# Summing two blocks of an adaLN projection on TensorE instead of VectorE in the first stage of a transformer block

## The chip, the cores and the metric

The kernel runs on one NeuronCore of a Trainium2 chip. It uses its engines TensorE (PE, matrix products into PSUM, with PEld for the loading of weights), VectorE (DVE), ScalarE (ACT), GpSimd (POOL) and SyncE (SP, which here issues nearly all DMA transfers). The metric is the device time of one execution in microseconds; the median of three runs is given. The profiler's trace is of one further execution.

## The reference

One layer of a hybrid encoder, batch 1, 512 tokens, 2048 features, everything in float32. From the conditioning vector c (2048 values) a modulation is computed, and the normalised input is scaled and shifted with it:

```python
c_act = jax.nn.silu(c)
mod = (c_act @ w_ada[i] + b_ada[i])[:, None, :]          # w_ada: 2048 x 12288
shift_m, scale_m, gate_m, shift_f, scale_f, gate_f = jnp.split(mod, 6, axis=-1)
h = rmsnorm(x, g_pre_mix[i]) * (1.0 + scale_m) + shift_m
y = token_mixer(h, w_in[i], ...)        # proj = h @ w_in, FoX attention + gated linear attention, @ w_out
x = x + gate_m * rmsnorm(y, g_post_mix[i])
h = rmsnorm(x, g_pre_mlp[i]) * (1.0 + scale_f) + shift_f
y = squared_relu_mlp(h, w_mlp_in[i], w_mlp_out[i])
x = x + gate_f * rmsnorm(y, g_post_mlp[i])
```

The change concerns scale_m and shift_m, 2048 columns of w_ada each, and the transpose of the normalised x.

## The kernel before

**The whole.** Each engine runs its own instruction list, written out by hand in one function per engine; semaphores order them. After a first stage the projection h @ w_in is computed in groups of six (later five) output tiles. Each float32 product is made of three matmuls on halves of the operands ("hi" and "lo", `split_mm`, lines 847 to 849). A group walks over 16 steps k, one for each 128 features. In a step TensorE makes 18 matmuls, and in a "slot" ahead of step k it does side work (`start_slot(2 * k)` in the first group). Later groups hold the attention in their slots; then follow the output projection and the MLP.

**The first stage, up to the first group.** SyncE issues in a fixed order: c, x in four token blocks, then w_ada in items (`load_am`, line 658), with weights of w_in between them. An item is 512 rows by 512 columns of w_ada, 1 MB in two transfers. Four items make a block of 512 columns. Blocks 0 to 3 are scale_m, blocks 4 to 7 shift_m, 32 items in all. Items lie in four buffers `am_item`; item n goes to buffer n % 4, so its load waits until item n - 4 is used (semaphore `am_used`). The first group's weights are loaded between items 18 and 31.

**Summing a block.** A matrix-vector product c_act @ w_ada is needed. DVE multiplies each row tile of an item with its column of c_act and adds it up in `am_acc` and `am_odd` (`add_am`, line 2094: 16 products and one sum, 17 instructions per block, `AM_BLOCK`). This leaves 128 partial rows. TensorE adds them over the partitions with a column of ones (`sum_columns`, line 1032), and DVE adds the bias (`mod_columns`, line 2158), which gives scale or shift for 512 features.

**x.** ScalarE squares each token block, GpSimd takes the inverse root, DVE scales blocks 0 to 2 and half of block 3, ScalarE the other half. Then TensorE transposes x, tile by tile (line 1020): all four token blocks of tile k into a PSUM bank (six banks, `TILES`), and ScalarE copies the bank to `xn_t` (line 1472).

**The fill.** While blocks of scale arrive one after the other, TensorE already computes the query part of the gated linear attention with the scale alone (`fill_unit`, line 1056). With it go the gate tiles (`gate_tiles`, line 1048): four matmuls at a time, each with 32 weight columns, each into its own 32 partitions of the bank BB, that is on four column strips of the array. The fill of block b needs scale block b.

**The first group.** It needs the last fill tile copied away, w_hi and w_lo of the first weights, and the modulated input of step k, so shift block k // 4. DVE's list there is: item 20, columns of block 4, item 21, `first_lo(0)` (line 2152), `modulated_pair(0)`, item 22 and so on (lines 2206 to 2240). Blocks 5, 6 and 7 of shift are summed in the slots 6, 14 and 22, ahead of the steps 3, 7 and 11; slot 28 holds the gate sums (lines 1095 to 1099).

Of the kernel before, what the change touches and what calls it, by code (L numbers as in the profile page):

```python
# [37 lines left out]
ALU = mybir.AluOpType  # L38
ACT = mybir.ActivationFunctionType
AX_X = mybir.AxisListType.X  # L40

P = 128
# [3 lines left out]
def build_block(nc, x, c, w_ada, b_ada, g_pre_mix, g_post_mix, w_in, b_fgate, w_gla_a2, b_gla_a2,  # L46
                g_fox_out, g_gla_out, w_out, g_pre_mlp, g_post_mlp, w_mlp_in, w_mlp_out, out):
    _, SEQ, D = x.shape
    KT = D // P
    TB = SEQ // P  # L50
# [22 lines left out]
    TILES = 6  # L73
# [21 lines left out]
    S_BLOCKS = KT // 4  # L95
    M_BLOCKS = 2 * S_BLOCKS
    F_ITEMS, G_ITEMS = KT // 2, KT // 4
    AM_BLOCK = 17
    F_USED = AM_BLOCK * M_BLOCKS
    G_USED = F_USED + FOX_GROUPS * F_ITEMS  # L100
    F_IN = 32 * M_BLOCKS
    G_IN = F_IN + 32 * FOX_GROUPS * F_ITEMS // 2
# [11 lines left out]
    with ExitStack() as ctx:  # L114
# [17 lines left out]
        x_raw = at("x_raw", [P, TB, D], R_A + 32 * KIB)  # L132
        x_junk = at("x_junk", [P, D], R_A)
        xn_t = at("xn_t", [P, KT, SEQ], R_B)
# [21 lines left out]
        am_item = [at(f"am_item{s}", [P, 4, 512], (R_AD, R_AD + 8 * KIB, R_G, R_G + 8 * KIB)[s]) for s in range(4)]  # L156
        am_acc = [at(f"am_acc{s}", [P, 512], (R_T + 12 * KIB, R_T + 14 * KIB, R_C + 6 * KIB)[s]) for s in range(3)]
# [342 lines left out]
        WARM_FILL = 10  # L500

        def items_used(n):
            return AM_BLOCK * (n // 4) + 4 * (n % 4)

        SPLIT_UNITS = (1, 3, 5, 7)

# [39 lines left out]
        def _(sp):  # L546
# [109 lines left out]


            def load_am(n):
                if n >= 4:
                    sp.wait_ge(am_used, items_used(n - 3))  # L660
                block, i = divmod(n, 4)
                col = (SCALE_M, SHIFT_M)[block // S_BLOCKS] + block % S_BLOCKS * 512
                for half in range(2):
                    k = 4 * i + 2 * half
                    sp.dma_start(am_item[n % 4][:, 2 * half:2 * half + 2, :], w_ada_t[:, k:k + 2, col:col + 512])\  # L665
                        .then_inc(am_in[n % 4], 16)
# [29 lines left out]
            def load_cumb(f):  # L696
                sp.wait_ge(ev_act, 3 * f + 1)
                for n in range(2):
                    sp.dma_start(cumb[n][:, :], cum_dram[bass.ds(2 * f + n, 1), :].to_broadcast([P, SEQ]))\
                        .then_inc(cumb_in, 16)  # L700

            F_AT = {0: (0,), 1: (1,), 2: (2, 3), 4: (4,), 5: (5,), 6: (6,), 7: (7,)}
            G_AT = {0: 0, 1: 1, 4: 2, 5: 3}

# [139 lines left out]
        def _(pe):  # L844
# [172 lines left out]
            pe.wait_ge(rows_in, 16 * 9)  # L1017
            pe.transpose(bank[5][:, 0:6 * KT], rows_a[:, :], ident[0:6 * KT, 0:6 * KT])
            pe.transpose(bank[5][:, 128:148], rows_b[:, :], ident[0:20, 0:20]).then_inc(rows_steps, 1)
            for k in range(KT):  # L1020
                if k == 0:
                    pe.wait_ge(xn_ready, TB)
                    pe.wait_ge(rows_steps, COLS_READY)
                if k == KT // 2:
                    pe.wait_ge(xn_right, 1)
                if k >= TILES:
                    pe.wait_ge(xt_act, k - TILES + 1)
                for t in range(TB):
                    last = pe.transpose(bank[k % TILES][:, t * P:t * P + P], x_raw[:, t, k * P:k * P + P], ident[:, :])
                last.then_inc(x_tr, 1)  # L1030

            def sum_columns(block):
                pe.wait_ge(am_used, items_used(4 * block + 4))
                if block:
                    pe.wait_ge(am_col, block)
                for j in range(4):
                    col = block // S_BLOCKS * 4 + j
                    last = pe.matmul(BA[:, col:col + 1], am_acc[block % 3][:, j * P:j * P + P], ones[:, 0:1],
                                     start=True, stop=True)
                last.then_inc(am_sum, 1)  # L1040

            sum_columns(0)
            for _ in range(WARM_FILL):
                pe.transpose(BB[:, 0:P], ident[:, :], ident[:, :])
            pe.wait_ge(xt_act, KT)
            FILL_SUMS = {3: 1, 7: 2, 11: 3, 14: S_BLOCKS}

            def gate_tiles(block):
# [33 lines left out]
            for block in range(S_BLOCKS):  # L1082
                pe.wait_ge(fill_in[block], 64)
                fill_unit(2 * block)
                fill_unit(2 * block + 1)

            FOX_SUMS = {6: S_BLOCKS + 1, 14: S_BLOCKS + 2, 22: S_BLOCKS + 3}

            def start_slot(s):
                if s in FOX_SUMS:  # L1090
                    sum_columns(FOX_SUMS[s])
                if s == 28:
                    pe.wait_ge(c_steps, C_ACT)
                    pe.wait_ge(gates_out, GATES_OUT)
                    pe.matmul(BB[0:32, :], gate_sel[:, :], gate_parts[:, :], start=True, stop=True)
                    pe.matmul(BB[32:40, :], gate_sel[:, RANK:RANK + FOX_HEADS], gate_parts[:, :], start=True, stop=True)
                    pe.wait_ge(g_ready, 1)
                    pe.matmul(BA[0:32, 8:9], g_sum[:, :], ones[:, 0:1], start=True, stop=True)
                    pe.matmul(BA[32:40, 8:9], g_sum[:, RANK:RANK + FOX_HEADS], ones[:, 0:1], start=True, stop=True)\
                        .then_inc(misc_sum, 1)  # L1100
# [214 lines left out]
        def _(act):  # L1315
# [143 lines left out]
            def scale_left(t):  # L1459
                cols = slice(0, D // 2)  # L1460
                act.wait_ge(x_rstd, t + 1)
                act.activation(x_raw[:, t, cols], x_raw[:, t, cols], ACT.Copy, scale=rstd[:, t:t + 1]).then_inc(xn_ready, 1)

            for t in range(TB):
                act.wait_ge(x_in[t], 16)
# [2 lines left out]
                act.activation(x_junk[:, :], x_raw[:, t, :], ACT.Square, accum_out=ss[:, t:t + 1]).then_inc(x_ss, 1)  # L1468
            scale_left(TB - 1)
            for k in range(KT):  # L1470
                act.wait_ge(x_tr, k + 1)
                act.activation(xn_t[:, k, :], bank[k % TILES][:, :], ACT.Copy).then_inc(xt_act, 1)

            def fill_operand(k):
                act.wait_ge(am_col, k // 4 + 1)
# [337 lines left out]
        def _(dve):  # L1813
# [280 lines left out]
            def add_am(n):  # L2094
                block, i = divmod(n, 4)
                total = am_acc[block % 3]
                dve.wait_ge(am_in[n % 4], 32 * (n // 4 + 1))
                if i == 0 and block >= 3:
                    dve.wait_ge(am_sum, block - 2)
                for j in range(4):  # L2100
                    part = (total, am_odd)[j % 2][:, :]
                    item, c_k = am_item[n % 4][:, j, :], c_act[:, 4 * i + j:4 * i + j + 1]
                    if i or j > 1 or (j and block):
                        dve.wait_ge(am_used, items_used(n) + j - 1)
                    if i or j > 1:
                        dve.scalar_tensor_tensor(part, item, c_k, part, ALU.mult, ALU.add).then_inc(am_used, 1)  # L2106
                    else:
                        dve.tensor_scalar(part, item, c_k, None, ALU.mult).then_inc(am_used, 1)
                if i == 3:
                    dve.wait_ge(am_used, items_used(n) + 4)  # L2110
                    dve.tensor_tensor(total[:, :], total[:, :], am_odd[:, :], ALU.add).then_inc(am_used, 1)
# [61 lines left out]
            def add_items(first, end):  # L2173
                for n in range(first, end):
                    add_am(n)
# [4 lines left out]

            scale_x(1)
            scale_x(2)
            add_am(0)
            scale_right(TB - 1)
            add_items(1, 4)
            mod_columns(0)
            fill_weights_lo(1)
            add_items(4, 6)
# [33 lines left out]
            add_am(27)  # L2222
            split_lo(4, 0, group_view)
            mod_columns(S_BLOCKS + 2)
            add_am(28)
            modulated_pair(8)
            add_items(29, 31)
            split_lo(5, 1, group_view)
            modulated_pair(10)
            add_am(31)  # L2230
            mod_columns(S_BLOCKS + 3)
            split_lo(6, 0, group_view)
            modulated_pair(12)
# [560 lines left out]
```

## Time and profile before

| | |
|---|---|
| median of three runs | 2189.64 us (2188.1 to 2189.9) |
| the profiled execution | 2188.36 us, span 2186.6 us |
| TensorE busy | 2152.3 us (98%) |
| DVE busy | 1545.3 us (71%) |
| ScalarE busy | 880.5 us (40%) |
| GpSimd busy | 362.9 us (17%) |
| moved by DMA | 445.46 MB, mean 204 GB/s |

The span is the profiled stretch; the execution's own time is 1.8 us longer. Busy shares are means over the whole span. Stages differ: in the first 100 us TensorE waits a good part of the time and the DMA engines are loaded, later it is the other way round. The views below therefore go by stretches and by waits. In a timeline a line gives start, duration, engine, line of the kernel, operation, output and inputs, shapes and count (x8: eight instructions merged; the duration is then that of them all), and in brackets the engine's idle time before it and what ended that. A float32 matmul shows as two matmul instructions, so a call to `pe.matmul` with float32 operands counts twice. A matmul's own duration holds its latency; the spacing of starts is what a matmul costs.

### The profile page before, as it was taken

The page shows a single profiled execution, that of the slowest core. Times are in us where ns is not written, and L with a number is a line of the kernel's source. Part 1 is how long each engine was busy: PE and PEld are TensorE (multiplying, and loading weights), DVE is VectorE, ACT ScalarE, POOL GpSimd, SP SyncE. Part 2 cuts the span into 40 slices and gives each one's busy share as a digit, 9 for nine tenths or more (in the row PEclk, how much of TensorE's full clock was granted, in tenths as well). Part 3 has the DMA queues.
Part 4 walks back from the last instruction along what each step waited for, and adds up shares of the span by engine and source line. Part 5 has one row for each costly group of instructions (what it writes and reads, how often), then busy time and mean ns, then how long its engine had stood idle before and what let it go on. Part 6 is the DMA issues. An engine that isn't in the chain of part 4 may idle for free.

```text
span 2186.6 us, 26836 instructions
## 1 busy us (share of the span) xinstructions
PE 2152.3 (98%) x9837; PEld 1754.0 (80%) x9837; DVE 1545.3 (71%) x1625; ACT 880.5 (40%) x1130; POOL 362.9 (17%) x206
## 2 busy tenths in 40 slices
PE   6999999999999999999999999999999999999998
PEld 4588888887777888888888888888888888888886
DVE  7987667677887626744554465445789898898988
ACT  5353333332343225543533434435444444444443
POOL 1000000000000001000000000000036455453634
PEclk9999999999999999999999999999999999999999
DMA  9966657655444443665675666655374765577764
GB/s 362 354 222 227 206 169 236 206 168 173 146 145 161 138 173 125 236 207 179 204 242 183 207 207 231 207 184 187 116 264 147 244 212 197 172 242 242 243 217 168
DMA packets 259333, 445.46 MB, mean 204 GB/s; under 512 B 18380, under 2 KB 102672, under 8 KB 253592
## 3 DMA queue, kind: packets, MB, share of 16 engines
q1 hardware_dynamic: 258976, 443.91, 60.5%
q8 instruction: 71, 1.16, 0.2%
q14 instruction: 38, 0.31, 0.0%
q10 hardware_dynamic: 248, 0.08, 0.0%
HBM read 384.14 MB, written 59.79 MB: 203 GB/s over the span
## 4 chain that ended last, share of the span: by engine, by line
PE 94%; DMA 2%; DVE 2%; issue 1%; SPq 1%; ACT 0%; DVEq 0%; POOL 0%; POOLq 0%
PE pair L847 30%; PE pair L849 30%; PE pair L848 30%; DMA am_item<-in_w_ada 2%; PE pair L948 1%; PE pair L922 1%; DVE am_acc L2106 0%; SPq L665 0%; DVE am_odd L2106 0%; PE pair L939 0%; PE pair L988 0%; PE pair L997 0%; PE pair L1151 0%; PE pair L889 0%; ACT y L1619 0%
## 5 line engine op out<-in xcount | busy, mean ns | idle before, releaser
L847 PE MATMUL pair<-in_hi,w_hi 128*128 128x512 f32 (+1 forms) x1728 | 689.6, 399 | 2.9 <-DVE in_lo L2134 2.8
L849 PE MATMUL pair<-in_hi,w_lo 128*128 128x512 f32 (+1 forms) x1728 | 670.9, 388 | 0.0
L848 PE MATMUL pair<-in_lo,w_hi 128*128 128x512 f32 (+1 forms) x1728 | 669.9, 388 | 0.0
L847 PEld LDWEIGHTS pair<-in_hi,w_hi 128*128 128x128 f32 x1728 | 324.7, 188 | 73.7 <-issue 10.1
L849 PEld LDWEIGHTS pair<-in_hi,w_lo 128*128 128x128 f32 x1728 | 324.4, 188 | 68.2
L848 PEld LDWEIGHTS pair<-in_lo,w_hi 128*128 128x128 f32 x1728 | 325.0, 188 | 64.8 <-issue 1.9
L847 PE MATMUL pair<-v_op,hid_r 128*128 128x512 f32 x896 | 348.7, 389 | 0.3 <-issue 0.3
L849 PE MATMUL pair<-v_op,hid_r 128*128 128x512 f32 x896 | 348.6, 389 | 0.0
L848 PE MATMUL pair<-v_op,hid_r 128*128 128x512 f32 x896 | 348.6, 389 | 0.0
L1826 DVE TENSOR_TENSOR w_lo<-w_raw,w_hi 128x2048 fp32r<-128x2048 f32 x62 | 144.7, 2334 | 287.5 <-ACT w_hi L1329 287.5
L2487 DVE TENSOR_TENSOR v_op<-v_raw,v_op 128x1024 fp32r<-128x1024 f32 x192 | 295.6, 1561 | 64.5 <-ACT v_op L1785 63.5
L1785 ACT ACTIVATE v_op<-v_raw 128x1024 fp32r<-128x1024 f32 x192 | 203.3, 1061 | 286.0 <-PE pair L849 268.0
L1329 ACT ACTIVATE w_hi<-w_raw 128x2048 fp32r<-128x2048 f32 x63 | 120.5, 1912 | 228.3 <-PE pair L849 228.3
L2752 POOL TENSOR_TENSOR v_sum<-v_raw,v_raw 128x512 f32<-128x512 f32 x60 | 149.2, 2513 | 367.8 <-DVE v_raw L2502 367.8
L847 PEld LDWEIGHTS pair<-v_op,hid_r 128*128 128x128 f32 x896 | 168.2, 188 | 35.8 <-ACT v_op L1785 0.7
L849 PEld LDWEIGHTS pair<-v_op,hid_r 128*128 128x128 f32 x896 | 168.2, 188 | 34.9
L848 PEld LDWEIGHTS pair<-v_op,hid_r 128*128 128x128 f32 x896 | 168.2, 188 | 34.9
L1818 DVE TENSOR_TENSOR w_lo<-w_raw,w_hi 128x1536 fp32r<-128x1536 f32 (+2 forms) x78 | 137.2, 1759 | 74.9 <-ACT w_hi L1320 74.0
L1320 ACT ACTIVATE w_hi<-w_raw 128x1536 fp32r<-128x1536 f32 (+2 forms) x78 | 116.0, 1487 | 177.6 <-PE pair L849 170.0
L2761 POOL TENSOR_TENSOR v_raw<-v_raw,v_sum 128x512 f32<-128x512 f32 x60 | 135.4, 2288 | 18.4 <-DVE v_op L2487 18.4
L2673 POOL TENSOR_TENSOR ada<-ada,c_act 128x2048 f32<-128x2048 f32 x8 | 31.4, 3926 | 587.8 <-DMA ada<-in_w_ada 552.4
L2543 DVE TENSOR_TENSOR y_t<-pair,y_t 128x1024 f32<-128x1024 f32 x104 | 125.0, 1215 | 0.7 <-PE pair L849 0.7
(283 smaller groups left out, 2289.5 us busy)
## 6 DMA issues: line engine op xcount, KB each, us to landing
w_raw<-in_w_mlp_in SPq DMA_DIRECT2D x64, 1024.0 KB, 5.3
v_raw<-in_w_mlp_out SPq DMA_DIRECT2D x128, 512.0 KB, 5.0
hid_r<-hid_scratch SPq DMA_DIRECT2D x112, 512.0 KB, 6.5
hid_scratch<-hid_r SPq DMA_DIRECT2D x28, 1792.0 KB, 8.3
am_item<-in_w_ada SPq DMA_DIRECT2D x64, 512.0 KB, 8.6
af_item<-in_w_ada SPq DMA_DIRECT2D x64, 512.0 KB, 4.7
w_raw<-in_w_in SPq DMA_DIRECT2D x96, 256.0 KB, 3.5
w_raw<-in_w_in SPq DMA_DIRECT2D x160, 128.0 KB, 3.4
```

Of the source, the lines that this page charges most:

```text
L847: pe.matmul(dst, a[0], b[0], start=start, stop=False, skip_group_check=onto)
L848: pe.matmul(dst, a[0], b[1], start=False, stop=False, skip_group_check=onto)
L849: return pe.matmul(dst, a[1], b[0], start=False, stop=stop, skip_group_check=onto)
L1320: act.activation(view(w_hi[n]), view(w_raw[n]), ACT.Copy).then_inc(hi_done, 1)
L1329: act.activation(m1_hi[m1_slot(j)][:, :], w_raw[j % 2][:, :], ACT.Copy).then_inc(hi_done, 1)
L1785: act.activation(v_op[i % 4][:, 0, :], raw_of(u, p)[:, h, :], ACT.Copy).then_inc(v_hi, 1)
L1818: dve.tensor_tensor(view(w_lo[n]), view(w_raw[n]), view(w_hi[n]).bitcast(F32), ALU.subtract)\
L1826: dve.tensor_tensor(m1_lo[m1_slot(j)][:, :], w_raw[j % 2][:, :], m1_hi[m1_slot(j)][:, :].bitcast(F32), ALU.subtract).then_inc(lo_done, 1)
L2487: dve.tensor_tensor(v_op[i % 4][:, 1, :], raw_of(u, p)[:, h, :], v_op[i % 4][:, 0, :].bitcast(F32), ALU.subtract).then_inc(v_lo, 1)
L2543: return dve.tensor_tensor(dst, src[:, :, :], dst, ALU.add)
L2752: last = pool.tensor_tensor(v_sum[:, h, cols], v_raw[q[B22]][:, h, cols], v_raw[q[B11]][:, h, cols], ALU.add)
L2761: last = pool.tensor_tensor(b21, b21, v_sum[:, h, cols], ALU.subtract)
```

## The change

Three edits belong together.

- **Blocks 0 and 7 are summed by TensorE** (`strip_sums`). For item i of the block it makes four matmuls, one for each row tile: the weights are one column of c_act repeated 32 times, the moving operand is the row tile (128 x 512 of float32). Row tile j goes to column strip j, partitions 32 j to 32 j + 31 of BB; the four items add up in PSUM. DVE then copies BB to `am_acc`, times 1/32 (`strips_out`), since each strip holds 32 equal rows, and `sum_columns` and `mod_columns` go on as before. DVE's products for items 0 to 3 and 28 to 31 are gone.
- **x is transposed by token blocks.** TensorE transposes token blocks 0 to 2 of the first six tiles as soon as each block is scaled. The last token block, and all four of the later tiles, follow. The sets for items 0, 1 and 2 stand ahead of tiles 0, 4 and 9, that for item 3 behind tile 15. Tiles 5, 7, 9, 11 and 13 are copied by DVE, the others by ScalarE.
- **Block 7** (items 28 to 31): the sets stand in the slots 16, 18 and 20 (two) of the first group, ahead of steps 8, 9 and 10. DVE copies them out behind `modulated_pair(10)`.

The buffers' waits follow: items 4 to 7 wait for the sets (`am0_used`) in place of DVE, and SyncE waits for all eight sets before it goes on to group 1. The order in which it issues is as it was. `am0_used` and `am0_sum` are further counts on semaphores already there.

```diff
-    F_USED = AM_BLOCK * M_BLOCKS
+    F_USED = AM_BLOCK * (M_BLOCKS - 2)
...
+        XT_DVE = (5, 7, 9, 11, 13)
...
             def load_am(n):
-                if n >= 4:
+                if n >= 8:
                     sp.wait_ge(am_used, items_used(n - 3))
+                elif n >= 4:
+                    sp.wait_ge(am0_used, AM0_USED + n - 3)
...
+            sp.wait_ge(am0_used, AM0_USED + 8)
...
+            def x_transpose(k, t):
+                return pe.transpose(bank[k % TILES][:, t * P:t * P + P], x_raw[:, t, k * P:k * P + P], ident[:, :])
+
+            def strip_sums(i, last_block=False):
+                if i == 0 and last_block:
+                    pe.wait_ge(gates_out, GATES_OUT)
+                elif i == 0:
+                    pe.wait_ge(c_steps, C_ACT)
+                pe.wait_ge(am_in[i], 32 * M_BLOCKS if last_block else 32)
+                for j in range(4):
+                    k = 4 * i + j
+                    last = pe.matmul(BB[32 * j:32 * j + 32, :], c_act[:, k:k + 1].to_broadcast([P, 32]),
+                                     am_item[i][:, j, :], start=(i == 0), stop=(i == 3))
+                last.then_inc(am0_used, 1)
+
+            for t in range(TB - 1):
+                pe.wait_ge(xn_ready, t + 1)
+                if t == 0:
+                    pe.wait_ge(rows_steps, COLS_READY)
+                for k in range(TILES):
+                    x_transpose(k, t)
+            SUMS_AHEAD = {0: 0, 4: 1, 9: 2}
             for k in range(KT):
+                if k in SUMS_AHEAD:
+                    strip_sums(SUMS_AHEAD[k])
...
                 if k >= TILES:
-                    pe.wait_ge(xt_act, k - TILES + 1)
-                for t in range(TB):
-                    last = pe.transpose(bank[k % TILES][:, t * P:t * P + P], x_raw[:, t, k * P:k * P + P], ident[:, :])
-                last.then_inc(x_tr, 1)
+                    xt_copied(pe, k - TILES)
+                    for t in range(TB - 1):
+                        x_transpose(k, t)
+                x_transpose(k, TB - 1).then_inc(x_tr, 1)
+            strip_sums(3)
...
+            STRIPS = {16: (0,), 18: (1,), 20: (2, 3)}
...
             def start_slot(s):
+                for i in STRIPS.get(s, ()):
+                    strip_sums(i, last_block=True)
                 if s in FOX_SUMS:
                     sum_columns(FOX_SUMS[s])
...
-            add_am(0)
             scale_right(TB - 1)
-            add_items(1, 4)
+            for k in XT_DVE:
+                dve.wait_ge(x_tr, k + 1)
+                dve.tensor_copy(xn_t[:, k, :], bank[k % TILES][:, :]).then_inc(xn_right, 1)
+            def strips_out(block, n):
+                dve.wait_ge(am0_used, AM0_USED + 4 * n)
+                dve.tensor_scalar(am_acc[block % 3][:, :], BB[:, :], 1.0 / 32, None, ALU.mult).then_inc(am0_sum, 1)
+
+            strips_out(0, 1)
             mod_columns(0)
...
-            add_am(28)
             modulated_pair(8)
-            add_items(29, 31)
             split_lo(5, 1, group_view)
             modulated_pair(10)
-            add_am(31)
+            dve.wait_ge(am_sum, S_BLOCKS + 1)
+            strips_out(M_BLOCKS - 1, 2)
             mod_columns(S_BLOCKS + 3)
```

## Rows read from the trace of the kernel before

**Rows 1.** busy time of the engines over the whole span, of the page (share, instructions)

```profile
PE 2152.3 (98%) x9837; PEld 1754.0 (80%) x9837; DVE 1545.3 (71%) x1625; ACT 880.5 (40%) x1130; POOL 362.9 (17%) x206
```

**Rows 2.** TensorE's waits from 98 us to the end: us in total, times, longest

```profile
PE pair L847 <- DVE in_lo L2134: 2.8, 1, 2.8
PE pair L1151 <- DVE y L2322: 0.5, 1, 0.5
```

**Rows 3.** chain of waits from 76 to 98.6 us: start, us, what

```profile
82.16 0.40 SPq L665
...
82.60 10.12 DMA am_item<-in_w_ada
...
92.74 0.75 DVE am_acc L2106
...
95.40 1.75 DVE w_lo L2155
97.15 0.61 DVE in_lo L2134
...
98.01 0.47 PE pair L847
```

**Rows 4.** stretches of 5 us: busy per engine, TensorE's clock, DMA share, GB/s

```profile
5.00:10.00 5.00, 0.00 (x0) 0.00 (x0) 0.60 (x3) 3.83 (x5) 0.21 (x2) 1.00 1.01 413
...
45.00:50.00 5.00, 5.00 (x15) 3.52 (x14) 3.37 (x7) 3.60 (x6) 0.00 (x0) 0.66 1.05 386
...
90.00:95.00 5.00, 5.00 (x24) 3.98 (x22) 4.20 (x9) 4.79 (x7) 0.00 (x0) 1.00 1.05 387
95.00:100.00 5.00, 2.24 (x11) 1.70 (x10) 5.00 (x7) 4.47 (x8) 0.00 (x0) 1.00 0.55 175
```

**Rows 5.** tile am_item to 170 us, what ended DVE's idle time (us, times)

```profile
  DMA am_item<-in_w_ada: 3.9, 7
```

**Rows 6.** timeline of all engines up to the first fill block

```profile
16.72 0.49 DVE L2108 TENSOR_SCALAR am_acc<-am_item,c_act 128x512 f32<-128x512 f32 x1 [0.70 <-DMA am_item<-in_w_ada]
...
18.48 8.90 PE L1029 MATMUL pair<-ident,x_raw 128*128 128x128 f32 x64 [6.84 <-ACT x_raw L1462]
...
25.13 0.75 DVE L2106 SCALAR_TENSOR_TENSOR am_acc<-am_item,c_act,am_acc 128x512 f32<-128x512 f32 x1 [0.24 <-DMA am_item<-in_w_ada]
...
28.40 1.19 ACT L1500 ACTIVATE fill_hi<-fill_w 128x1024 fp32r<-128x1024 f32 x1
28.65 1.05 PE L1038 MATMUL pair<-ones,am_acc 128*128 128x1 f32 x8 [1.27 <-DVE am_acc L2111]
...
30.18 2.56 ACT L1476 ACTIVATE in_tmp<-xn_t,mod_a 128x512 f32<-128x512 f32 x4 [0.59 <-DVE mod_a L2169]
```

**Rows 7.** the same timeline, TensorE in the first fill block

```profile
31.05 3.67 PE L1075 MATMUL pair<-in_tmp,fill_w 128*128 128x512 f32 x8 [0.19 <-ACT in_tmp L1476]
...
34.65 1.07 PE L1052 MATMUL pair<-in_tmp,wm_raw 128*32 128x512 f32 x8
...
35.64 3.70 PE L1075 MATMUL pair<-in_tmp,fill_w 128*128 128x512 f32 x8
```

**Rows 8.** timeline of TensorE at the sums of block 7 and the gates

```profile
144.88 0.95 PE L1038 MATMUL pair<-ones,am_acc 128*128 128x1 f32 x8
...
157.84 0.39 PE L849 MATMUL pair<-in_hi,w_lo 128*128 128x512 f32 x1
158.16 0.62 PE L1095 MATMUL pair<-gate_parts,gate_sel 128*32 128x512 f32 x1
...
159.17 0.50 PE L847 MATMUL pair<-in_hi,w_hi 128*128 128x512 f32 x1
159.51 0.40 PE L848 MATMUL pair<-in_lo,w_hi 128*128 128x512 f32 x1
```

**Rows 9.** timeline of SyncE, the issue of item 31

```profile
130.49 0.94 SPq L665 DMA_DIRECT2D am_item<-in_w_ada  x2
```

**Rows 10.** timeline of DVE, a copy of a bank with a scalar

```profile
167.19 0.69 DVE L1836 TENSOR_SCALAR grp<-pair 128x512 f32<-128x512 f32 x1
```

More of the change, by code:

```diff
@@ L502, in items_used, with xt_copied @@
         def items_used(n):
-            return AM_BLOCK * (n // 4) + 4 * (n % 4)
+            return AM_BLOCK * (n // 4 - 1) + 4 * (n % 4)
+        am0_used, AM0_USED = c_in, 16
+        am0_sum, AM0_SUM = rows_in, 16 * 9 + 1
+        XT_DVE = (5, 7, 9, 11, 13)
+        x3_left = 1
+        def xt_copied(engine, k):
+            if k in XT_DVE:
+                engine.wait_ge(xn_right, 2 + XT_DVE.index(k))
+            else:
+                engine.wait_ge(xt_act, x3_left + len([n for n in range(k + 1) if n not in XT_DVE]))
         SPLIT_UNITS = (1, 3, 5, 7)
@@ L1019, in _ @@
             pe.transpose(bank[5][:, 128:148], rows_b[:, :], ident[0:20, 0:20]).then_inc(rows_steps, 1)
+            def x_transpose(k, t):
[18 more added lines that the diff above has]
+            SUMS_AHEAD = {0: 0, 4: 1, 9: 2}
             for k in range(KT):
+                if k in SUMS_AHEAD:
+                    strip_sums(SUMS_AHEAD[k])
                 if k == 0:
-                    pe.wait_ge(xn_ready, TB)
-                    pe.wait_ge(rows_steps, COLS_READY)
+                    pe.wait_ge(xt_act, x3_left)
                 if k == KT // 2:
@@ L1026, in _ @@
                 if k >= TILES:
-                    pe.wait_ge(xt_act, k - TILES + 1)
-                for t in range(TB):
-                    last = pe.transpose(bank[k % TILES][:, t * P:t * P + P], x_raw[:, t, k * P:k * P + P], ident[:, :])
-                last.then_inc(x_tr, 1)
-            def sum_columns(block):
-                pe.wait_ge(am_used, items_used(4 * block + 4))
+                    xt_copied(pe, k - TILES)
[3 more added lines that the diff above has]
+            strip_sums(3)
+            def sum_columns(block):
+                if block == 0:
+                    pe.wait_ge(am0_sum, AM0_SUM)
+                elif block == M_BLOCKS - 1:
+                    pe.wait_ge(am0_sum, AM0_SUM + 1)
+                else:
+                    pe.wait_ge(am_used, items_used(4 * block + 4))
                 if block:
@@ L1044, in _ @@
                 pe.transpose(BB[:, 0:P], ident[:, :], ident[:, :])
-            pe.wait_ge(xt_act, KT)
+            xt_copied(pe, KT - 1)
+            xt_copied(pe, XT_DVE[-1])
             FILL_SUMS = {3: 1, 7: 2, 11: 3, 14: S_BLOCKS}
@@ L1461, in scale_left @@
                 act.wait_ge(x_rstd, t + 1)
-                act.activation(x_raw[:, t, cols], x_raw[:, t, cols], ACT.Copy, scale=rstd[:, t:t + 1]).then_inc(xn_ready, 1)
+                act.activation(x_raw[:, t, cols], x_raw[:, t, cols], ACT.Copy, scale=rstd[:, t:t + 1]).then_inc(xt_act, 1)
             for t in range(TB):
@@ L1470, in _ @@
             for k in range(KT):
-                act.wait_ge(x_tr, k + 1)
-                act.activation(xn_t[:, k, :], bank[k % TILES][:, :], ACT.Copy).then_inc(xt_act, 1)
+                if k not in XT_DVE:
+                    act.wait_ge(x_tr, k + 1)
+                    act.activation(xn_t[:, k, :], bank[k % TILES][:, :], ACT.Copy).then_inc(xt_act, 1)
+            xt_copied(act, XT_DVE[-1])
             def fill_operand(k):
@@ L2102, in add_am @@
                     item, c_k = am_item[n % 4][:, j, :], c_act[:, 4 * i + j:4 * i + j + 1]
-                    if i or j > 1 or (j and block):
+                    if items_used(n) + j > 1:
                         dve.wait_ge(am_used, items_used(n) + j - 1)
```

## The prediction

> **What bounds the kernel now.** The page's busy row comes first: TensorE is busy for 2152.3 of 2186.6 us [rows 1]. Next the waits of TensorE from 98 us to the end: the 2.8 us at 98 are the only wait of weight, and from there on TensorE runs through [rows 2]. So the time is the start of that run (98.01 us) plus what TensorE has to do in it plus a tail. A change gains if it brings the start forward, and loses whatever it adds to TensorE behind it, one for one.
>
> What sets the start? The chain back from 98.01 reads: in_lo (DVE, 97.15), w_lo (95.40), the four products of block 5's item 21 from 92.74, that item's transfer of 10.12 us, and before it SyncE's issue at 82.16, released by DVE [rows 3]. Read quickly, this says that a quicker DVE would issue item 21 sooner and so land it sooner. The windows say otherwise: from 5 to 95 us the DMA share is at or above 1.01 in each of the 18 stretches of 5 us; 45:50 and 90:95 both show 1.05 at 386 and 387 GB/s, and only 95:100 falls to 0.55 [rows 4]. A transfer that takes 10.12 us while 387 GB/s flow has about 3.9 MB in front of it (itself included): it stands in a line that never empties. The order of the line is SyncE's program order, which the change leaves as it is. So item 21 lands at about 92.7 whatever DVE does earlier, and the order "item 21, first w_lo, first in_lo" on DVE stays too.
>
> **The change, part by part.**
>
> *Block 0 leaves DVE (items 0 to 3).* Before: item 0 is taken up at 16.72, item 3 at 25.13 on landing, the columns are summed by TensorE at 28.65, and ScalarE starts the fill operand at 30.18 [rows 6]. After: of the 64 transposes (8.90 us from 18.48, so 0.139 each [rows 6]) the 18 of token blocks 0 to 2 for the first six tiles lie in TensorE's idle time before 18.48, and so does the set for item 0, there at 16.72. The other 46 stay: 46 x 0.139 = 6.4 us. Among them stand the sets for items 1 to 3. The nearest row for a set is the gate tiles: the same four column strips, 512 columns of float32, eight instructions; from their start to the next matmul it is 35.64 - 34.65 = 0.99 us [rows 7]. A set that waits for its item holds the transposes behind it: from 16.72 to 25.13 the items come some 2.8 us apart, so item 2 at about 22.3, and TensorE is at its set after 18 transposes and a set, 18.48 + 2.5 + 0.99 = 22.0; it waits 0.3. Then DVE copies the sums out of PSUM; the nearest row is 0.69 us for 128x512 with a scalar [rows 10]. From 18.48: 6.4 + 3 x 0.99 + 0.3 + 0.69 = 10.4, so the column sums start at 28.9 against 28.65: no change to speak of. The earliest end is item 3's landing, 25.13 + 0.99 + 0.69 = 26.8, 1.8 us sooner; but the operands of the fill are only split from 28.40 [rows 6]. The late end, with sets and transposes at half speed, is 18.48 + 2 x 9.4 + 0.69 = 38. I take 28.9, since the speed of both is measured in this very stage.
>
> What either end is worth at 98 us: DVE waits 3.9 us in all for landings of these items, in seven places, of which 0.70 (item 0) and 0.24 (item 3) lie in block 0 [rows 5, 6]. The other 2.9 us lie between block 0 and the start. An earlier front lengthens these waits; a later one eats them first. So from 1.8 us early to 2.9 us late the start stays. Cost taken: 0.
>
> *Copies out of PSUM.* Five of sixteen go from ScalarE to DVE, which now has nothing else there; behind them only the 0.69 us copy waits. Nothing at 98 us.
>
> *Loads of items 4 to 7* wait for sets, not for DVE. The sets come in the same order and within about a microsecond of DVE's products, and the line in front of the DMA engines is some 10 us deep [rows 3]. Nothing. Were that cover gone, a late set for item 3 would delay item 7 by as much, still inside the 2.9 us.
>
> *Block 7 leaves DVE (items 28 to 31), and four sets go into the run that never waits.* DVE loses 17 instructions around 128 to 144 us, which nobody waits for [rows 2]. TensorE gets one set before step k = 8, one before k = 9, two before k = 10. A step takes (144.88 - 98.01 - 2 x 0.95) / 11 = 4.09 us [rows 3, 8], so a matmul 4.09 / 18 = 0.227. The cost of a change of form in this run is seen at the gate sums: after 157.84 the next start was due at 158.07 and came at 158.16 (0.09); behind them the first matmul took 159.51 - 159.17 = 0.34 in place of 0.227 (0.11) [rows 8]. A single set: 0.09 + 0.99 + 0.11 = 1.19; the double one 0.09 + 1.98 + 0.11 = 2.18. Sum: 2 x 1.19 + 2.18 = 4.56 us. The low end is 4 x 0.99 = 3.96; a gain is excluded because TensorE has no idle time there to be filled. The high end is four strips one after the other: four matmuls of 128 columns take 34.65 - 31.05 = 3.60 us in eight instructions [rows 7], four sets 14.4 us. I take 4.56: the gate tiles differ from a set only in that the 32 weight columns are one column repeated.
>
> The Trainium skill has a rule on packed tiles: its page "TensorE: Matmul & The Clock Gate" (section "Measured speedup vs the span model") gives 3.07 times for four packed tiles, where the rows here make 3.60 / 0.99 = 3.6 times. By that rule of the Trainium skill a set would be 3.60 / 3.07 = 1.17 and the sum, as an estimate, 5.3 us; the measured rows go first.
>
> *New waits there.* The double set waits for item 31, issued at 130.49 to 131.43 [rows 9]; even with 10.12 us to land it is there at 141.6. Step 10 starts at 144.88 - 4.09 = 140.8, plus two sets 143.2. The first set's wait for the gate sums is long past, as these are copied during the fill. Nothing. DVE waits for the double set before it copies; queued behind are block 7's columns, a w_lo and two in_lo, which in both kernels cannot start before the columns are summed at the head of step 11. That sum shifts with TensorE, so their distance to step 12 stays. SyncE's new wait for all sets ends around 145, before the first w_raw of group 1 is free, which takes the w_lo queued behind block 7's columns. Nothing.
>
> **The sum.** Start 0, run +4.56, tail 0. The profiled execution took 2188.36 us (span 2186.6), 1.28 below the median of the three runs, so it would become 2192.9; a median of runs should move with it: 2189.64 + 4.56 = 2194.2. That is 0.21%, right at what a measurement of this kernel can tell from no change (0.2%, 4.4 us).
>
> **Rivals.**
> 1. *The line of transfers has room: not slower.* If the rate would rise when SyncE is released sooner, DVE would no longer wait for landings: 2.9 us, plus at most 1.8 us from the front, brings the start 4.7 us forward, to 93.3 (the fill's own matmuls end at 98.01 - 2.8 = 95.2 [rows 2, 3], so 2.8 is what remains): +4.56 - 2.8 = +1.8, so 2191.4. For it: the chain, which goes through SyncE's wait. Against it: the share of 1.05 without a gap. The Trainium skill, page "DMA: Bandwidth & Descriptors" (section "Where 436 GB/s comes from"), puts the ceiling of the ports at 435 GB/s; worked out from that figure, 387 would leave 11% of room, as an estimate. The trace goes to 413 GB/s while x is loaded, at a share of 1.01, and to 387 at 1.05 with the items [rows 4], so here that room is not seen to be usable. To be faster than before by 0.2% the start would have to come 9 us sooner, before the fill can end.
> 2. *Strips don't run side by side.* With repeated weights, or four different moving operands, a set costs 3.60: +14.4 us, 2204. For: no row shows repeated weights. Against: the gate tiles' four operands differ as well.
> 3. *The front slips.* If sets and transposes ahead of the fill run at half speed for most of the time, block 0 is late by more than the 2.9 us of waits behind it; each microsecond beyond them comes on top. With 2 us beyond: 2196.2. For: TensorE's granted clock is 0.66 in 45:50 [rows 4], so this stage does lose speed. Against: that stretch costs the start nothing now.
> 4. *The change doesn't tell*: the sets would have to lie in idle time of TensorE from 132 to 145, and 2189.6 would stay. There is none [rows 2].
>
> **Chances.** Forecast 0.70 (own range 2193.0 to 2195.5), rival 1 0.14, rival 2 0.04, rival 3 0.10, rival 4 0.02. The range of 8 in 10 takes in most of rivals 1 and 3: 2190.2 to 2197.0. The forecast lies across the bound of 0.2%: 0.39 of it slower, 0.31 the same. Rivals 2 and 3 add 0.12 to slower and 0.02 to the same, rival 1 gives 0.11 to the same and 0.03 to faster, rival 4 0.02 to the same. Slower 0.51, same 0.46, faster 0.03; I give faster 0.05 for what I don't see, at the cost of the same.
>
> **What would show it.** Item 21 still lands near 92.7 and the run starts between 97.5 and 98.5 (rival 1: before 97, and DMA above 390 GB/s). Four sets in the run, each 0.9 to 1.2 us from its first start to the next in_hi matmul (rival 2: over 3). TensorE without a wait between 98 and 170. DVE idle for some 11 us in 128 to 146. The prediction is wrong if the start moves by over 1 us, or if a wait of TensorE appears behind a set.

## The result and the profile after

The changed kernel takes 2193.66 us, the median of 15 runs (2192.98 to 2195.37), against 2189.43 for the kernel before in the same comparison (15 runs, 2188.02 to 2190.31): ratio 1.0022, 95% interval 1.0015 to 1.0029. That is 4.23 us slower, where the prediction said 4.56 and 2194.2. The profiled execution has a span of 2191.2 us, 4.6 more than before.

Busy time of the engines from the page, which answers to [rows 1]: TensorE has 64 matmuls more, the eight sets of eight; DVE has 27 instructions less.

```profile
PE 2163.7 (99%) x9901; PEld 1755.2 (80%) x9901; DVE 1528.2 (70%) x1598; ACT 878.6 (40%) x1125; POOL 361.8 (17%) x206
```

TensorE's waits from 98 us on (total, times, longest), for [rows 2]. The start of the run is still released by in_lo on DVE, now after 2.0 us in place of 2.8. No wait stands behind a set. One of 0.5 us at L953, among the attention's matmuls later on, is new to the list.

```profile
PE pair L861 <- DVE in_lo L2184: 2.0, 1, 2.0
PE pair L953 <- ACT prob L1436: 0.5, 1, 0.5
```

The chain of waits from 76 to 98.6 us, for [rows 3]. It no longer passes through a transfer or SyncE: it comes through the fill on TensorE and reaches DVE's products of item 21. The step from TensorE to DVE at 94.49 is no wait, though: DVE's products start back to back there (93.83, 94.49) and DVE is not idle before them. The run still starts at 97.76 (before 98.01).

```profile
81.15 3.67 PE pair L1120 x8
...
94.49 0.75 DVE am_odd L2156
...
96.82 0.70 DVE in_lo L2184
...
97.76 0.47 PE pair L861
```

Stretches of TensorE's clock, DMA share and GB/s (the last three columns), for [rows 4]: the line of transfers is as full as it was, up to 95 us. New is the clock in the first fill block, 0.74 and 0.92, where the kernel before was granted 1.00 in both stretches; that one had its low stretch later (0.66 in 45:50), where the changed kernel has 1.00.

```profile
30.00:35.00 5.00, 4.78 (x21) 3.14 (x22) 3.81 (x8) 3.44 (x6) 0.00 (x0) 0.74 1.05 386
35.00:40.00 5.00, 5.00 (x17) 1.74 (x16) 3.59 (x6) 0.15 (x1) 0.00 (x0) 0.92 1.09 351
...
90.00:95.00 5.00, 5.00 (x25) 4.18 (x25) 4.85 (x10) 4.34 (x6) 0.00 (x0) 1.00 1.05 385
95.00:100.00 5.00, 3.02 (x14) 2.19 (x13) 5.00 (x7) 4.84 (x9) 0.00 (x0) 1.00 0.59 180
```

The timeline up to the first fill block, for [rows 6, 7] (start, length, engine and line, [idle before]). The sets of items 0 and 1 take 1.94 and 1.89 us, those of items 2 and 3 1.06. Six transposes at 16.06 take 1.54. The column sums stand at 30.03 (before 28.65), and the first half of the fill block takes 5.36 (before 3.67).

```profile
16.06 1.54 PE L1036 MATMUL pair<-ident,x_raw 128*128 128x128 f32 x6 [0.54 <-DVE x_raw L2165]
...
17.53 1.94 PE L1046 MATMUL pair<-am_item,c_act 128*32 128x512 f32 x8
...
20.44 1.89 PE L1046 MATMUL pair<-am_item,c_act 128*32 128x512 f32 x8
...
23.95 1.06 PE L1046 MATMUL pair<-am_item,c_act 128*32 128x512 f32 x8
...
28.15 1.06 PE L1046 MATMUL pair<-am_item,c_act 128*32 128x512 f32 x8
...
30.03 1.05 PE L1082 MATMUL pair<-ones,am_acc 128*128 128x1 f32 x8 [0.81 <-DVE am_acc L2239]
...
32.42 5.36 PE L1120 MATMUL pair<-in_tmp,fill_w 128*128 128x512 f32 x8 [0.18 <-ACT in_tmp L1526]
```

The tile am_item to 170 us, for [rows 5]: DVE no longer waits for any landing. Its line there (3.9 us, seven times) is gone, and no other has taken its place.

TensorE's timeline at the first and the last slot with sets and at the sums of block 7, for [rows 8]. A single set is 133.52 - 132.52 = 1.00 us to the next matmul, the double one 144.97 - 143.12 = 1.85. From the start of the run to the sums of block 7 it is 149.21 - 97.76 = 51.45 us; before it was 144.88 - 98.01 = 46.87.

```profile
132.20 0.39 PE L863 MATMUL pair<-in_hi,w_lo 128*128 128x512 f32 x1
132.52 1.06 PE L1046 MATMUL pair<-am_item,c_act 128*32 128x512 f32 x8
133.52 0.50 PE L861 MATMUL pair<-in_hi,w_hi 128*128 128x512 f32 x1
133.85 0.39 PE L862 MATMUL pair<-in_lo,w_hi 128*128 128x512 f32 x1
...
142.80 0.39 PE L863 MATMUL pair<-in_hi,w_lo 128*128 128x512 f32 x1
143.12 1.92 PE L1046 MATMUL pair<-am_item,c_act 128*32 128x512 f32 x16
144.97 0.50 PE L861 MATMUL pair<-in_hi,w_hi 128*128 128x512 f32 x1
145.31 0.40 PE L862 MATMUL pair<-in_lo,w_hi 128*128 128x512 f32 x1
...
149.21 0.94 PE L1082 MATMUL pair<-ones,am_acc 128*128 128x1 f32 x8
```

DVE's timeline. Its first in_lo waits 1.41 us for TensorE's fill, which it did not before, and the last sum of block 1 stands at 45.47. Item 21 is taken up at 92.49 without a wait for its landing. DVE idles 7.54 us before the copy of block 7's sums and 4.32 behind it.

```profile
38.84 1.29 DVE L2199 TENSOR_TENSOR in_lo<-in_tmp,in_hi 128x512 fp32r<-128x512 f32 x2 [1.41 <-PE pair L1097]
...
45.47 0.69 DVE L2161 TENSOR_TENSOR am_acc<-am_acc,am_odd 128x512 f32<-128x512 f32 x1
...
92.49 0.75 DVE L2156 SCALAR_TENSOR_TENSOR am_acc<-am_item,c_act,am_acc 128x512 f32<-128x512 f32 x1
...
145.18 0.69 DVE L2239 TENSOR_SCALAR am_acc<-pair 128x512 f32<-128x512 f32 x1 [7.54 <-PE pair L1046]
150.19 0.16 DVE L2221 TENSOR_TENSOR mod_b<-pair,cols_a 128x4 f32<-128x4 f32 x1 [4.32 <-PE pair L1082]
```

The same sum of block 1 in DVE's timeline of the kernel before:

```profile
42.88 0.69 DVE L2111 TENSOR_TENSOR am_acc<-am_acc,am_odd 128x512 f32<-128x512 f32 x1
```

### The profile page after: what moved, and what is told of

It is laid out like the page before. It is cut to its first block, busy times and chain, and to the rows that moved or that the text cites. A ratio compares the mean times of both kernels' runs of the same rounds, so it can differ in the third digit from the quotient of the medians.

```text
span 2191.2 us, 26931 instructions
## 1 busy us (share of the span) xinstructions
PE 2163.7 (99%) x9901; PEld 1755.2 (80%) x9901; DVE 1528.2 (70%) x1598; ACT 878.6 (40%) x1125; POOL 361.8 (17%) x206
## 4 chain that ended last, share of the span: by engine, by line
PE 96%; DVE 1%; issue 1%; ACT 1%; DMA 0%; DVEq 0%; POOL 0%; SPq 0%; POOLq 0%; ACTq 0%
PE pair L861 30%; PE pair L863 30%; PE pair L862 30%; PE pair L1120 1%; PE pair L962 1%; PE pair L936 1%; PE pair L1046 0%; PE pair L953 0%; PE pair L1002 0%; PE pair L1011 0%; PE pair L1036 0%; PE pair L1199 0%; PE pair L903 0%; PE pair L1082 0%; DMA w_raw<-in_w_in 0%
```

## The experiments

The theory: the start of the run is set by item 21's landing and the order on DVE behind it, so the relief of DVE at block 0 is worth nothing; the loss is the four sets of block 7, one for one. The rivals: the line of transfers has room and the start can be had by a quicker DVE; or the loss is in what the sets do to their neighbours, not in the sets.

**Each half alone.** Block 0 by sets and block 7 on DVE as before (against the changed kernel, its core):

```
-            STRIPS = {16: (0,), 18: (1,), 20: (2, 3)}
+            STRIPS = {}
...
+            add_am(28)
             modulated_pair(8)
+            add_items(29, 31)
             split_lo(5, 1, group_view)
             modulated_pair(10)
-            dve.wait_ge(am_sum, S_BLOCKS + 1)
-            strips_out(M_BLOCKS - 1, 2)
+            add_am(31)
```

> Only the first half of the change: block 0 by sets on TensorE with x transposed by token blocks; block 7 stays on DVE. Theory (the line of transfers sets the start of the run, the sets in the run are the whole loss): start between 97.5 and 98.3, TensorE's work in the run as before, so 2189.4 within 1 us of the kernel before. Rival (DVE's chain sets the start and block 0's relief is worth something): start 1.5 to 2.8 us earlier, 2186.6 to 2188. Second rival (the late front costs): start after 99, over 2190.5.

Measured: 2189.32 us, ratio 1.0001 (0.9992 to 1.001), span 2186.6 as before. The sets of items 0 and 1 are slow here too (1.94, 1.79), the column sums stand at 29.88, and the start at 97.76. The first half of the first fill block takes 3.67 us, as in the kernel before, and DVE still waits for item 21. TensorE's timeline, then DVE's:

```profile
32.27 3.67 PE L1118 MATMUL pair<-in_tmp,fill_w 128*128 128x512 f32 x8 [0.19 <-ACT in_tmp L1524]
```

```profile
92.49 0.75 DVE L2154 SCALAR_TENSOR_TENSOR am_acc<-am_item,c_act,am_acc 128x512 f32<-128x512 f32 x1 [0.32 <-DMA am_item<-in_w_ada]
```

Block 7 by sets, block 0 and the transposes as in the kernel before (against the changed kernel, its core):

```
             def load_am(n):
-                if n >= 8:
+                if n >= 4:
                     sp.wait_ge(am_used, items_used(n - 3))
-                elif n >= 4:
-                    sp.wait_ge(am0_used, AM0_USED + n - 3)
...
+            add_am(0)
             scale_right(TB - 1)
...
-            strips_out(0, 1)
+            add_items(1, 4)
```

> Only the second half: block 7 by four sets in the slots 16, 18 and 20, block 0 and the transposes as before. Theory: start at 98.0, sums of block 7 at 149.4 (144.88 + 4.56), time +4.6: 2194.0. Rival (the loss comes from the front or from something between): time within 1 us of before, and the loss in the run of the first half alone.

Measured: 2193.04 us, ratio 1.002 (1.0011 to 1.0029), span 2191.1. From its start at 97.85 to the sums of block 7 at 149.26 it is 51.41 us. Against the kernel before it is 4.5 us by the spans and 3.46 by the medians of this comparison. So the whole loss lies in block 7; block 0 neither adds to it nor takes from it by more than the interval of the first half, 0.1% or about 2 us, can show.

**Is it the landing?** Half the bytes of each item from item 4 on are left out:

```
-                    sp.dma_start(am_item[n % 4][:, 2 * half:2 * half + 2, :], w_ada_t[:, k:k + 2, col:col + 512])\
+                    rows = 1 if n >= 4 else 2
+                    sp.dma_start(am_item[n % 4][:, 2 * half:2 * half + rows, :], w_ada_t[:, k:k + rows, col:col + 512])\
```

> The kernel before, but from item 4 on each transfer of an item brings one row tile of its two, so half the bytes; all products are still made, half of them on rows left over from earlier items. Theory (a full line of transfers sets the start): items land earlier, DVE's 2.9 us of waits for landings between block 0 and the start vanish, and the start falls to 95 to 96. Rival (DVE's chain alone sets the start): 98.0 as before.

Measured: 2184.88 us in one run, with the kernel before at 2189.64 beside it. TensorE's timeline has the start 3.4 us sooner (a little below the 95 to 96 expected), still behind DVE:

```profile
94.65 0.47 PE L848 MATMUL pair<-in_hi,w_hi 128*128 128x512 f32 x1 [1.72 <-DVE in_lo L2135]
```

With half the bytes gone DVE has no wait for a landing behind block 0, so its own work is the next bound, some 3.4 us away. The weights stand in the same line and come sooner too, so this run moves more than item 21. The other side is a quicker DVE with the line as it is: two of four products of an item on 16 columns in place of 512, from item 4 on:

```
-                    part = (total, am_odd)[j % 2][:, :]
-                    item, c_k = am_item[n % 4][:, j, :], c_act[:, 4 * i + j:4 * i + j + 1]
+                    cols = slice(0, 16 if n >= 4 and j > 1 else 512)
+                    part = (total, am_odd)[j % 2][:, cols]
+                    item, c_k = am_item[n % 4][:, j, cols], c_act[:, 4 * i + j:4 * i + j + 1]
```

> The kernel before, but from item 4 on the products with the third and fourth row tile of an item take 16 of 512 columns, so DVE has about 1.1 us less to do per item, some 20 us before the start; the transfers are unchanged. Theory (the line sets the start): item 21 is taken up at 92.5 to 92.9, and the start is the landing plus the shorter work, 96.5 to 97.2. Rival (DVE's chain sets the start): item 21 is taken up well before 92, and the start comes at the end of the fill, 94 or earlier.

Measured: 2187.12 us in one run. DVE's waits for landings rise from 3.9 to 21.2 us, and its timeline shows item 21 taken up on landing, at nearly the same time as before (92.74). DVE's timeline, then TensorE's:

```profile
92.59 0.75 DVE L2107 SCALAR_TENSOR_TENSOR am_acc<-am_item,c_act,am_acc 128x512 f32<-128x512 f32 x1 [2.86 <-DMA am_item<-in_w_ada]
94.21 1.75 DVE L2156 TENSOR_TENSOR w_lo<-w_raw,w_hi 128x1536 fp32r<-128x1536 f32 x1
```

```profile
96.82 0.47 PE L847 MATMUL pair<-in_hi,w_hi 128*128 128x512 f32 x1 [1.10 <-ACT gg L1493]
```

The start, 96.82, comes 1.19 us sooner, as w_lo does (94.21 in place of 95.40): 0.15 of it is the landing, the rest what the shorter products of item 21 itself save. The row names ScalarE's copy of a fill tile as what ended the wait, so here the end of the fill would not have let the run start sooner either. A DVE that is quicker earlier waits longer and lands nothing sooner by more than 0.15 us: the prediction's reading against rival 1 holds.

**The order behind the landing.** In the kernel before, item 21 is put behind the first w_lo and the first in_lo:

```
-            add_am(21)
             first_lo(0)
-            modulated_pair(0)
+            modulated_lo(0)
+            add_am(21)
+            modulated_lo(1)
```

> The kernel before with one edit on DVE's list: item 21 is added up between the two first in_lo in place of ahead of the first w_lo, so the start no longer waits for that item's landing. Theory (landing of item 21 plus the work behind it on DVE sets the start): the start falls to the end of the fill and its copies, 95.2 to 95.8, time 2.2 to 2.8 us lower: 2186.6 to 2187.2. Rival (DVE has that much to do in any order): the start stays at 97.5 to 98, time as before.

Measured: 2186.53 us, ratio 0.9987 (0.9978 to 0.9996), span 2184.7: better than both kernels. TensorE's timeline: the fill and the run join without a wait; a smaller one of 0.88 us appears 18 us later, and the sums of block 7 stand 1.78 us sooner than before.

```profile
94.72 0.39 PE L849 MATMUL pair<-in_hi,fill_lo 128*128 128x512 f32 x1
94.95 0.39 PE L847 MATMUL pair<-in_hi,w_hi 128*128 128x512 f32 x1
...
113.49 0.47 PE L847 MATMUL pair<-in_hi,w_hi 128*128 128x512 f32 x1 [0.88 <-DVE in_lo L2134]
...
143.10 0.94 PE L1038 MATMUL pair<-ones,am_acc 128*128 128x1 f32 x8
```

The same move on the kernel with block 0 by sets (against the first experiment; the same lines):

```
-            add_am(21)
             first_lo(0)
-            modulated_pair(0)
+            modulated_lo(0)
+            add_am(21)
+            modulated_lo(1)
```

> The first half of the change (block 0 by sets, block 7 on DVE) together with item 21 between the two first in_lo. Theory: block 0's relief adds nothing to the reordering; start 95.2 to 96, time 2186.6 to 2187.6, the same as the reordering alone. Rival (relief of DVE shows once the landing is out of the way): 1 us or more below the reordering alone.

Measured: 2187.53 us, ratio 0.9991 (0.9982 to 1.0), span 2186.0; the first matmul of the run at 95.72, the sums of block 7 at 143.74. With the landing out of the way, the late front is no longer free: it costs 143.74 - 143.10 = 0.64 us, since the fill itself ends later (its last matmul starts at 95.50, against 94.72).

And on the changed kernel:

```
-            add_am(21)
             first_lo(0)
-            modulated_pair(0)
+            modulated_lo(0)
+            add_am(21)
+            modulated_lo(1)
```

> The changed kernel with item 21 of block 5 put behind the first w_lo and the first in_lo on DVE, nothing else. Theory (start of the run and the sets in it add up): the start of the run comes forward as in the kernel before with the same move (there the time fell by 2.9 us of its 2189.4, the sums of block 7 by 1.8 us), less up to 1 us since the front with sets is late by 1.4 us; the four sets still cost 4.6 us: 2191.0 to 2192.0. Rival (the two share a cause): the time falls to that of the kernel before or below, under 2189.7, or doesn't fall, over 2193.

Measured: 2192.51 us, ratio 1.0017 (1.0008 to 1.0026), half a microsecond above the range expected; its profiled execution took 2191.85. The sums of block 7 stand at 148.26, 4.52 us behind the 143.74 of the kernel without sets in the run. So the order moves the start, the sets cost their time behind it, and the two add. The order gains less on the changed kernel, though: 1.15 us by the medians and 1.2 by the spans, against 3.05 and 1.9 in the kernel before.

**The front at full speed.** Transposes of the unit matrix, 62 in all (the expectation counts 67), keep TensorE busy ahead of the sets (against the changed kernel, its core):

```
+            def warm(n):
+                for _ in range(n):
+                    pe.transpose(BA[:, 0:P], ident[:, :], ident[:, :])
...
+            warm(36)
...
+                warm((6, 5, 10)[t])
...
+            warm(5)
```

> The changed kernel with 67 transposes of the identity in TensorE's idle time ahead of the sets for items 0 and 1, so that it is busy from about 3 us on. Theory (the front does not matter, and it came late because those sets ran at half speed): each set takes about 1.0 us, block 0's column sums start at 28.2 to 28.6 in place of 30.03, DVE waits for landings again, and the start stays at 97.5 to 98. Rival (the late front set the start in the changed kernel): start 1.5 us earlier.

Measured: 2193.98 us in one run. The sets take 1.06 us each, but the column sums come at 29.37, not 28.2 to 28.6, because the set of item 2 waited for its landing; and the start slipped to 99.35, which no theory had. TensorE's timeline, then DVE's:

```profile
23.29 1.07 PE L1052 MATMUL pair<-am_item,c_act 128*32 128x512 f32 x8 [1.27 <-DMA am_item<-in_w_ada]
...
97.83 0.39 PE L863 MATMUL pair<-in_hi,fill_lo 128*128 128x512 f32 x1
...
99.35 0.47 PE L861 MATMUL pair<-in_hi,w_hi 128*128 128x512 f32 x1 [1.14 <-ACT gg L1551]
```

```profile
94.09 0.75 DVE L2164 SCALAR_TENSOR_TENSOR am_acc<-am_item,c_act,am_acc 128x512 f32<-128x512 f32 x1 [0.21 <-DMA am_item<-in_w_ada]
```

Item 21 was taken up 1.6 us later here, on landing, and the start came 1.6 us later. That does not show that the start followed the landing: the last matmul of the fill started at 97.83, against 95.40 in the changed kernel, and the row of the start names ScalarE's copy of a fill tile as what ended the wait. So the expectation on the front was met only in part and the one on the start missed, and why both the line and the fill were later in this execution is open.

**All four sets in one slot** (against the changed kernel):

```
-            STRIPS = {16: (0,), 18: (1,), 20: (2, 3)}
+            STRIPS = {20: (0, 1, 2, 3)}
```

> The changed kernel with all four sets of block 7 in one slot ahead of step k = 10, in place of one ahead of k = 8, one ahead of k = 9 and two ahead of k = 10. Theory (the loss is TensorE's own time: 4 sets, and a change of form for every slot): the changes of form are paid once instead of three times, so start of the run to sums of block 7 goes from 51.45 to 51.0 us (four sets 3.6 to 3.8 us from the first set to the next in_hi matmul), time some 0.4 us below the changed kernel, 2193.2. Rival (the loss is in what the slots do to the neighbouring steps or to DVE, not in the sets): 51.45 stays, or the wait for item 31 or for the copy shows up as a wait of TensorE, 2193.7 or more.

Measured: 2193.83 us, ratio 1.0022 (1.0013 to 1.0031): no difference from the changed kernel that the times can tell, and not the 2193.2 of the theory but where the rival had it. Its trace, though, answers two questions. First the slot, in TensorE's timeline: four sets take 145.83 - 142.26 = 3.57 us to the next matmul, 0.89 each.

```profile
16.23 0.88 PE L1036 MATMUL pair<-ident,x_raw 128*128 128x128 f32 x6 [0.54 <-DVE x_raw L2165]
17.05 1.06 PE L1046 MATMUL pair<-am_item,c_act 128*32 128x512 f32 x8
...
19.67 1.07 PE L1046 MATMUL pair<-am_item,c_act 128*32 128x512 f32 x8 [0.52 <-DMA am_item<-in_w_ada]
...
28.46 1.05 PE L1082 MATMUL pair<-ones,am_acc 128*128 128x1 f32 x8 [0.81 <-DVE am_acc L2239]
...
97.78 0.77 PE L861 MATMUL pair<-in_hi,w_hi 128*128 128x512 f32 x1 [2.11 <-DVE in_lo L2184]
...
101.25 0.39 PE L863 MATMUL pair<-in_hi,w_lo 128*128 128x512 f32 x1
...
142.26 3.64 PE L1046 MATMUL pair<-am_item,c_act 128*32 128x512 f32 x32
145.83 0.50 PE L861 MATMUL pair<-in_hi,w_hi 128*128 128x512 f32 x1
...
150.04 0.95 PE L1082 MATMUL pair<-ones,am_acc 128*128 128x1 f32 x8
```

From the start to the sums of block 7 it is 52.26 us, not 51.0. But eight matmuls at the start took 101.25 - 97.78 = 3.47 us, where the changed kernel's took 99.69 - 97.76 = 1.93: 1.54 us were lost there, to the clock (below). Without them the run would be 50.72, 0.73 less than with three slots. That the saving is the sets' is a reading of one trace; the times don't show it, so the rival isn't excluded by them.

Second, this execution had the same front code, but its sets ran at full speed from the first, and its column sums stood at 28.46, 1.57 us ahead of the changed kernel's 30.03. DVE's timeline shows what became of it: a wait for item 21's landing, which ends where the changed kernel began without one (92.49).

```profile
92.52 0.75 DVE L2156 SCALAR_TENSOR_TENSOR am_acc<-am_item,c_act,am_acc 128x512 f32<-128x512 f32 x1 [0.27 <-DMA am_item<-in_w_ada]
```

The start is 97.78 against 97.76. One and a half microseconds at the front are worth nothing at 98 us, as the prediction had it.

## Why the prediction was right

*Start of the run, 97.5 to 98.5:* 97.76, and 97.76 to 97.85 in the two halves. The reason given (a full line of transfers, item 21 near 92.7 whatever DVE does) is borne out by the two sides of it: fewer bytes move the start, less work on DVE before item 21 moves its landing by 0.15 us at most. With item 21 behind the first in_lo the run starts at the end of the fill.

*Block 0, column sums at 28.9:* 30.03, so this step was mis-sized by 1.1 us. Part of rival 3 came true: six transposes and two sets ran at half speed, (1.54 - 0.88) + (1.94 - 1.06) + (1.89 - 1.07) = 2.4 us more than in the execution of the one-slot kernel, where the same code ran at full speed and met the forecast to 0.4 us (28.46). The waits of 2.9 us behind block 0 covered it, but something that the prediction didn't have drew on them too: the granted clock of 0.74 and 0.92 in the first fill block. The first half of that block took 5.36 - 3.67 = 1.69 us longer, DVE's in_lo waited 1.41 us behind it, and DVE was done with block 1 at 45.47 against 42.88: 2.59 us late, of which the column sums account for 1.38. After that no wait for a landing was left on DVE. It took up item 21 at 92.49 without one, where the landing ended a wait in two other kernels (92.49 with block 0 alone by sets, 92.52 in the one-slot kernel): its own list had become as late as the landing. The reasoning was right, and that the start held in this execution was luck in the margin: a front later still would, by this account, have come on top, which no run shows.

*Four sets, 4.56 us:* from the last regular matmul to the second one behind the slot, less two regular steps of 0.227, the single slots cost 133.85 - 132.20 - 0.45 = 1.20 (forecast 1.19) and the double one 145.31 - 142.80 - 0.45 = 2.06 (forecast 2.18). A second set behind a first is cheaper than 0.99 (0.85 here). Sum 4.46; the run as a whole grew by 4.58. The rest, 0.12, lies between the slots: behind each, the matmuls stand wider for a while: (147.40 - 145.31) / 9 = 0.232 apart over the nine from 145.31 on, in place of 0.227.

*Strips side by side:* yes, with the repeated column as with the gate tiles; rival 2 is out. The Trainium skill, page "TensorE: Matmul & The Clock Gate" (section "Measured speedup vs the span model"), would have made a set 1.17 us, as an estimate from its 3.07 times, which it gives for four row tiles, not column strips; the trace has 1.00.

*No wait behind a set, and some 11 us of idle DVE in 128 to 146:* no such wait is there, and DVE is busy for 5.29 of these 18 us, so idle for 12.7, of which 7.54 in one piece.

*Tail 0:* from the sums of block 7 to the end it is 2191.2 - 149.21 = 2041.99 against 2186.6 - 144.88 = 2041.72. The traces of the eleven kernels differ by more than that among themselves (2041.39 with the front at full speed, 2042.26 in the one-slot kernel), so the 0.27 us isn't shown to be the change's. The wait at L953 (0.5) goes with it in part: it is 0.2 and 0.3 in the kernels with one half of the change, and 0.7 where item 21 is moved with block 0 by sets; what makes ScalarE late there was not looked into. In all: -0.25 + 4.58 + 0.27 = 4.6.

*The time, 2194.2:* 2193.66. The spans of two executions agree with the sum (4.6). That the medians come as close (4.23 against 4.56) is partly chance, since the runs of the kernel before fall into two heaps 1.8 us apart (last section) and its median moves with the share of each: 2189.43 in this comparison, 2188.47 in the last.

The prediction had one thing in hand and didn't use it: the order on DVE that makes TensorE wait for item 21, which the run at 98 doesn't need. Changing that order gained 3.05 us by the medians (1.9 by the spans) in the kernel before and 1.15 (1.2) in the changed one; taking work off DVE ahead of the landing gained nothing that the times can tell.

## What to carry to other kernels

When an engine is taken to be late because of its own work, look at what it waited for: if transfers stand in a line that never empties, relief in front of the landing turns into waiting, and what counts is the order of the work behind it. Work moved onto an engine that never waits is paid in full, so price it from the nearest row of that same stage, change of form included, and expect little else. And when a forecast leans on slack behind a step, count how much of the slack is left afterwards, not only whether it was enough.

## What the runs showed of the hardware

*The clock at the start of a run differs between executions of one code.* TensorE idles for about 2 us at 98 in most of these kernels. In the one-slot kernel the granted clock behind that idle time was 0.77 in 95:100 and 0.89 in 100:105, with eight matmuls 0.43 us apart in place of 0.23, at the lower level of 1.2 GHz; in the changed kernel (1.98 us idle) and the kernel before (2.76) it stayed at 1.00. Windows of the one-slot kernel:

```profile
95.00:100.00 5.00, 2.89 (x8) 2.04 (x8) 5.00 (x7) 4.76 (x8) 0.00 (x0) 0.77 0.61 185
100.00:105.00 5.00, 5.00 (x21) 4.06 (x20) 5.00 (x8) 0.00 (x0) 0.00 (x0) 0.89 0.94 284
```

The first fill block shows the same: the changed kernel and the one with block 0 alone by sets have the same code up to there, but the first half of that block took 5.36 us in the one, with 0.74 granted in 30:35, and 3.67 in the other, with 1.00.

The runs of the kernel before fall into two heaps, their means 1.8 us apart (in the last comparison 14 from 2187.97 to 2188.72 and 7 from 2189.75 to 2190.94), and ten of the eleven runs of the reordered kernel before, which has no wait at 98, lie within 0.84 us (2186.11 to 2186.95). That fits a clock which sometimes falls in that wait (1.54 us were lost to it in the one-slot kernel), and would explain why the median fell by 3.05 us where the span fell by 1.9. But the two other kernels without that wait spread wider, ten of eleven runs over 1.29 us (block 0 by sets) and 1.65 us (the changed kernel reordered), so that clock can't be the only source of spread; with traces of single executions it isn't shown.

*The column of the clock doesn't tell all.* At 16 to 22 us the changed kernel's sets ran at half speed, while the granted clock reads 1.00 there; it first shows a lower value at 30:35 (0.74). The length of known instructions (1.94 us for a set there, 1.06 later) is the surer sign in that stretch.
